# Two blocks of a transformer: half of the memory's values computed in another stage

## The reference, cut to what matters

```python
mx = split((silu_c @ w_mod[l] + b_mod[l]), 6)              # shifts, scales and gates of a layer
zx = modulate(rms_norm(x, norm1_g[l]), mx[0], mx[1]) @ w_in[l]
...                                                        # mixers, w_o
x  = x + mx[2] * mixer_rest(...)
hx = modulate(rms_norm(x, norm2_g[l]), mx[3], mx[4])       # the layer's second norm
x  = x + mx[5] * square(relu(hx @ w_mlp1[l])) @ w_mlp2[l]
...
# second block, much later
mem_n = rms_norm_2(mem, norm_mem)
kv = (mem_n @ xa_wkv).reshape(B, M, 2, 4, 256)             # keys: first 1024 columns, values: last 1024
```

## Time and profile before

| | us |
|---|---|
| median of 3 runs (lowest, highest) | 1874.79 (1873.02, 1876.01) |
| the profiled execution | 1872.94 |
| its span, from the first to the last instruction | 1871.1 |
| TensorE busy in the span | 1764.5 (94%) |
| VectorE, ScalarE, GpSimd busy | 925.8, 398.6, 298.0 |
| mean granted TensorE clock | 0.982 |

### The profile page before, as it was taken

How to read it: one execution, slowest core, us unless ns; L and a number is a source line. 1 busy time by engine, 2 the same in 40 slices (tenths; PEclk the granted TensorE clock), 3 DMA queues, 4 the chain that set the end, 5 groups by cost and what they waited for, 6 DMA issues and landing times.

```text
span 1871.1 us, 25901 instructions
## 1 busy us (share of the span) xinstructions
PE 1764.5 (94%) x10456; PEld 1391.1 (74%) x10456; DVE 925.8 (49%) x1738; ACT 398.6 (21%) x757; POOL 298.0 (16%) x305
## 2 busy tenths in 40 slices
PE   7999999899999999899899999977999899999997
PEld 5434444488888888656899987855798688888886
DVE  1247542464676434575687643299621432255511
ACT  1312444221112210346221002210421101200000
POOL 0100252122001211005243110166000000000000
PEclk9999999999999999999999999888999999999999
DMA  7774483122333222321354554222312344244443
GB/s 291 308 288 185 161 323 127 67 71 88 113 135 113 81 79 88 112 68 52 130 179 159 177 180 138 91 95 108 113 48 92 113 158 135 91 158 153 144 154 112
DMA packets 38704, 256.22 MB, mean 137 GB/s; under 512 B 4128, under 2 KB 7328, under 8 KB 9024
## 3 DMA queue, kind: packets, MB, share of 16 engines
q1 hardware_dynamic: 36240, 240.86, 36.9%
q0 software_dynamic: 1776, 9.57, 1.3%
q10 hardware_dynamic: 576, 4.19, 0.5%
HBM read 247.27 MB, written 7.34 MB: 136 GB/s over the span
## 4 chain that ended last, share of the span: by engine, by line
PE 78%; DVE 13%; ACT 2%; DMA 2%; issue 2%; POOL 2%; SPq 0%; ACTq 0%; DVEq 0%; POOLq 0%
PE ps L595 77%; DMA ring<-weights 1%; DVE arena L1869 1%; PE ps L790 1%; DVE arena L2027 1%; DMA xT<-x_t 1%; DVE arena L2067 1%; DVE spare L2140 1%; DVE arena L2066 1%; POOL aux L1672 0%; DVE aux L1899 0%; DVE arena L1900 0%; DVE arena L1901 0%; ACT hT L1322 0%; POOL aux L1655 0%
## 5 line engine op out<-in xcount | busy, mean ns | idle before, releaser
L595 PE MATMUL ps<-hT,ring 128*128 128x256 f32 (+3 forms) x3184 | 739.6, 390 | 22.7 <-issue 17.0
L595 PEld LDWEIGHTS ps<-hT,ring 128*128 128x128 f32 (+1 forms) x3184 | 571.3, 193 | 181.3 <-issue 111.2
L595 PE MATMUL ps<-arena,ring 128*128 128x256 f32 (+3 forms) x1884 | 380.2, 358 | 5.0 <-DVE arena L1901 3.2
L595 PEld LDWEIGHTS ps<-arena,ring 128*128 128x128 f32 (+1 forms) x1884 | 317.6, 190 | 58.7 <-issue 13.3
L1655 POOL TENSOR_TENSOR aux<-aux 128x256 f32<-128x256 f32 (+1 forms) x46 | 50.0, 1088 | 611.0 <-ACT aux L1257 543.0
L595 PE MATMUL ps<-arena,sums 128*128 128x256 f32 (+1 forms) x768 | 136.5, 327 | 1.3 <-DVE aux L1965 1.3
L595 PEld LDWEIGHTS ps<-arena,sums 128*128 128x128 f32 x768 | 118.2, 191 | 12.3 <-DVE aux L1965 2.5
L1257 ACT ACTIVATE aux<-xT 128x256 f32<-128x256 f32 (+1 forms) x64 | 31.0, 494 | 285.7 <-DVE xT L2057 93.3
L1672 POOL TENSOR_SCALAR aux<-aux,small 128x512 f32<-128x512 f32 (+1 forms) x48 | 70.8, 1483 | 117.8 <-DVE small L1917 117.7
L1691 POOL TENSOR_TENSOR arena<-arena 128x256 f32<-128x256 f32 (+1 forms) x32 | 27.0, 843 | 332.4 <-ACT arena L1442 332.4
L595 PE MATMUL ps<-hT,sums 128*128 128x128 f32 (+1 forms) x512 | 78.6, 301 | 0.7 <-DVE aux L1965 0.4
(11 more groups left out here) (334 smaller groups left out, 1831.8 us busy)
## 6 DMA issues: line engine op xcount, KB each, us to landing
ring<-weights SPq DMA_DIRECT2D x224, 1024.0 KB, 4.9
kept_turns<-aux ACTq DMA_DIRECT2D x4, 1024.0 KB, 5.7
arena<-kept_turns POOLq DMA_DIRECT2D x6, 512.0 KB, 4.6
kept_keys_values<-spare POOLq DMA_DIRECT2D x1, 2048.0 KB, 8.2
arena<-kept_keys_values POOLq DMA_DIRECT2D x1, 2048.0 KB, 8.1
tab<-tables SPq DMA_DIRECT2D x1, 1344.0 KB, 13.7
arena<-mem_t SPq DMA_DIRECT2D x2, 512.0 KB, 5.7
xT<-ctx_t SPq DMA_DIRECT2D x1, 1024.0 KB, 9.2
```

The costliest lines, as they stand in the source:

```text
L595: ins = nc.tensor.matmul(o_, lhsT, rhs, start=start, stop=stop, skip_group_check=True)
```

## The change

The last 512 columns of the values (`values(1)`) leave the opening stage. Their two chunks now stand between the last chunk of `w_o` and the first of layer 0's MLP. TensorE does them in three parts, behind tile 7 of `w_o` and in the two steps after it. In the opening stage `mod_block(0, 3)` now stands ahead of `values(0)`, and `mod_turn(0, 0)` and norm 0's statistic stand inside it. GpSimd adds four of the squares of norm 0 and TensorE takes the other four. ScalarE and VectorE take their steps in the order that this gives. The first half of the values and the keys are stored by two transfers (1 MB, and 0.5 MB in pieces of 2 KB). The late half is copied to free memory and stored by two transfers of ScalarE's queue. `ctmp` moves, so that the normalized memory stays whole until then.

```diff
-SUMMED = {0: 7, 1: 7, 2: 6, 3: 7, 4: 6, 6: 7, 7: 7, 8: 7}
+SUMMED = {0: 4, 1: 7, 2: 6, 3: 7, 4: 6, 6: 7, 7: 7, 8: 7}
...
     keys(6, 8)
+    mod(0, 3)
     values(0)
-    mod(0, 3)
-    values(1)
...
+        if l == 0:
+            whole()
+            values(1)
         whole()
         for what, hf, p, g, n in mlp_order(l):
...
-        ctmp = flat[:, o:o + 1024].rearrange("p (n t) -> p n t", n=2)
-        assert o + 1024 <= 16 * 1024
+        ctmp = flat[:, 4608:4608 + 1024].rearrange("p (n t) -> p n t", n=2)
+        assert o <= 56 * T
...
+        late_values = (rawf[:, 0:512], auxf[:, 6144:6656])
...
             mem_keys(6, 8)
-            mem_values(0, 0, KD)
+            mod_block(0, 3)
+            mem_values(0, 0, 2)
+            mod_turn(0, 0)
+            mem_values(0, 2, 4)
             for k in range(KD):
                 norm_stat_step(("st", 0), 0, k, slice(0, 2 * T))
-            mod_block(0, 3)
-            mem_values(1, 0, 2)
-            mod_turn(0, 0)
-            mem_values(1, 2, KD)
+            mem_values(0, 4, KD)
...
                     if n >= 2:
                         norm_stat_step(("st", 2 * l + 1), 2 * l + 1, n - 2, s)
+                    if l == 0 and n >= KD - 1:
+                        mem_values(1, *((0, 2), (2, 4), (4, KD))[n - KD + 1])
...
-                    did(f(first_v[:, tt * D + half * 512:tt * D + half * 512 + 512], bank(key), ACT.Copy), key=key, wait=False)
+                    if half == 0:
+                        did(f(first_v[:, tt * D:tt * D + 512], bank(key), ACT.Copy), key=key, wait=False)
+                    else:
+                        dst = late_values[tt]
+                        did(f(dst, bank(key), ACT.Copy), key=key)
+                        act.dma_start(kept[:, 2 + tt, 512:1024], dst).then_inc(S["values_kept"], 16)
...
-            mem_values_out(0)
-            root(("st", 0), rinv, slice(0, 2 * T), 1.0 / D)
...
             mod_rows_out(0, 0)
+            root(("st", 0), rinv, slice(0, 2 * T), 1.0 / D)
...
                     modulated(0, 0, 0, 0, (0, 1))
-                    mem_values_out(1)
+                    mem_values_out(0)
...
-                    act.wait_ge(S["mem_kept"], 16)
+                    act.wait_ge(S["mem_kept"], 32)
...
+                if l == 1:
+                    act.wait_ge(S["values_kept"], 32)
...
                 modulated_halves(l)
                 if l == 0:
+                    mem_values_out(1)
                     did(f(small2[:, 0, :], cols("s5_log_step_2", 0, S5T), ACT.Exp), "s5_act")
...
-            for half in range(2):
-                for tt_ in range(2):
-                    taken(pool, ("xv", half, tt_))
-            pool.dma_start(kept, spare[:, :, :]).then_inc(S["mem_kept"], 16)
-            pool.wait_ge(S["mem_kept"], 16)
+            for n in range(KD):
+                taken(pool, ("xk", n))
+            for tt_ in range(2):
+                taken(pool, ("xv", 0, tt_))
+            pool.dma_start(kept[:, 0:2, :], spare[:, 0:2, :]).then_inc(S["mem_kept"], 16)
+            pool.dma_start(kept[:, 2:4, 0:512], spare[:, 2:4, 0:512]).then_inc(S["mem_kept"], 16)
+            pool.wait_ge(S["mem_kept"], 32)
...
+            pool.wait_ge(S["values_kept"], 32)
             pool.dma_start(arena[:, 9:13, :], kept).then_inc(S["mem_back"], 16)
...
+            mods(0, 0, 0, 4 * MOD_FIRST)
             scaled(0, slice(0, 2 * T), ("st", 0))
-            mods(0, 0, 0, 4 * MOD_FIRST)
             for l in range(LAYERS):
                 s = side(l)
+                if l == 1:
+                    dve.wait_ge(S["values_kept"], 32)
```

More of the change, by code:

```diff
@@ L499, in two_blocks @@
                   "q_nope", "max_ready", "prob_ready", "sum_ready", "conv_scaled", "conv_done", "conv_centred", "conv_act", "hidden",
-                  "x1_square", "x1_root", "h2_ready", "s5_loaded", "mem_loaded0", "mem_loaded1", "mem_squares", "mem_ready", "mem_kept", "mem_back", "scaled",
+                  "x1_square", "x1_root", "h2_ready", "s5_loaded", "mem_loaded0", "mem_loaded1", "mem_squares", "mem_ready", "mem_kept", "values_kept", "mem_back", "scaled",
                   "gla_dve", "gla_act", "gla_done", "s5_act", "s5_dve", "s5_turn", "s5_tabs", "s5_scanned", "s5_states", "s5_spilled0", "s5_spilled1", "s5_back0", "s5_back1",
```

## The result

The changed kernel takes 1886.97 us (median of 4 runs, 1884.66 to 1889.3) against 1874.89 us (median of 4 runs as well, one more than were known before); the ratio is 1.0066, 95% interval 1.0054 to 1.0079. That is 12.1 us slower, where +9.8 was forecast with a range of 1879.8 to 1888.0. The profiled execution took 1888.15 us, 15.2 more than the one of before.

The account below looks back on a forecast made before the run. TensorE, busy 94% of the span, was taken as the bound, so its work and idle time count. Opening +0.6 and end of w_o +9.15 gave +9.8 us, 1884.6 as a median, range 1879.8 to 1888.0.

Parts of the forecast that it names:

- The opening's gap: Opening stage, behind the fourth w_mod block: TensorE idle 10.7 us from 50.9, until chunk 12 lands at 61.6.
- The clock's part: Opening, behind TensorE's long idle time: lower clock costs 2.0 us, between nothing and 2.7.
- The end of `w_o`: Layer 0, tile 7: VectorE's wait for chunk 68 and four additions delay the norm's chain and forms, +9.15 us.
- the third rival: End of w_o: VectorE not held by chunk 68, only TensorE's order counts; +6.2, in all +6.8, 1881.6; chance 0.07.
- some 5 us twice: Sign expected in the profile after: VectorE's L1941 waits some 5 us twice in `residual`.
- the start of the z tiles: Opening: first modulated tile at 79.8 doesn't bind; z tiles start at 83.0, 0.7 us earlier than before.
- The stores beside the chunk loads: z tiles: key and value stores compete with needed chunks, costing nothing to 2.5 us, taken as 1.3.
- +0.6: The opening's sum: -0.7 for the earlier z start, +1.3 for stores beside chunk loads.
- the second rival: Opening loses more: clock low for 5 us of full work, store takes its whole share; about +12, 1887; chance 0.10.

Follow-up runs that it names:

- tables_late: Changed kernel with SyncE's load of the tables (1.3 MB) behind chunk 13 instead of ahead of chunk 12; 1884.35 us, ratio 1.0053.
- fill_gap: Changed kernel with 20 extra matmuls in TensorE's gap behind the fourth w_mod block, into a bank later overwritten; one execution, 1888.16 us.
- hold_after_tile: Changed kernel with weight_sums of the MLP's second chunk behind the addition of w_o's tile 7 in layer 0; 1884.30 us, ratio 1.0051.
- gains_early: Changed kernel with VectorE forming the gain of layer 0's first norm ahead of the eight scaled tiles; 1882.52 us, ratio 1.0032.
- values_behind: Changed kernel with all late values behind the last statistic step and weight_sums of the second MLP chunk behind the scaled tiles; 1882.38 us, ratio 1.0033.
- both_repaired: Changed kernel with gain ahead of scaled tiles, all late values behind the last statistic step, second MLP chunk's weight_sums behind scaled tiles; 1874.46 us, ratio 0.9997.

## Why the prediction was right, point by point

**Which way, and why: right.** The opening's gap was forecast at 10.7 us from 50.9, and was 9.63 from 51.7. It is the queue ahead of chunk 12: tables_late moved it by the tables' share. The clock's part, taken as 2.0 us from a row of another stage, was 1.6 (5.32 against 3.68, and 3.70 in fill_gap).

**The end of `w_o`: right in place and nearly in size.** +9.15 was forecast and +8.45 came. The issue came 1.2 us behind the values' start, the landing took 4.7 us, and the four additions took 2.8, all a little under the rows used. The wait of VectorE's queue for chunk 68 was the mechanism. But it isn't alone: the order on TensorE by itself costs what the third rival said (+6.2; hold_after_tile came to +5.9). Two slips of the text change no sum: it announces a wait of VectorE of "some 5 us twice", where its own times give some 9 us for the second (4.98 and 9.90 came), and the MLP's first two chunks were one and two behind tiles 6 and 7, not both two.

**The step that failed: the start of the z tiles.** The forecast as a whole came true, but this step of it didn't. The text says that with one tile scaled and two modulations the first tile comes 5.8 us behind the statistic, at 79.8, and that this "doesn't bind". The modulations wait for `gain` as well, and VectorE forms that behind all eight tiles, 4.9 us of work. Before the change the same order stood there and cost nothing, because TensorE had values to do until 83.67; the earlier trace rows even name `gain` as what ended ScalarE's wait, and I read only the length of that row. The first modulated tile thus came at 85.6, not 79.8. That is 3.8 us of idle time and then a first z tile at the low clock, 10.10 us in place of 7.03. gains_early removes both.

**The term that was too large.** The stores beside the chunk loads were given 1.3 us. In the changed kernel TensorE waited for no chunk there, as z itself was late. With z at 81.2 the wait was 1.60 us, so there is such a wait and the term belongs to the kernel that I had in mind, not to this one. That kernel is gains_early: its place behind the z tiles (`mod_turn(0, 1)`) stands at 162.05 against 162.29, so -0.2 where +0.6 was forecast. In all the change's opening cost +5.2.

**Where the rest went.** By the trace the two places make +5.2 and +8.5, 13.7 together, and the median moved by 12.1. Between the z tiles and `w_o` this execution won back 3.0 us. That stretch (from `mod_turn(0, 1)` to the end of tile 7) took 188.3 to 194.7 us in the twelve profiled executions, with the same work in it, and was the second longest, 194.5, in the one of before. The rows account for 2.5 of the 3.0. At one place TensorE waits 1.05 us twice for VectorE in both kernels, and the eight records behind it took 5.23 us before and 3.70 after:

```profile
196.75 5.23 PE L595 MATMUL ps<-ring,arena 128*128 128x512 f32 x8 [1.05 <-DVE arena L1901]
...
270.66 1.06 PE L595 MATMUL ps<-ring,sums 128*32 128x512 f32 x6 [1.28 <-DMA ring<-weights]
```

```profile
201.89 3.70 PE L598 MATMUL ps<-ring,arena 128*128 128x512 f32 x8 [1.05 <-DVE arena L1918]
...
235.47 1.06 PE L598 MATMUL ps<-ring,sums 128*32 128x512 f32 x6 [0.32 <-DMA ring<-weights]
```

That is 1.5 us, at a granted clock of 0.83 from 190 to 200 us before and 1.00 in the changed kernel. Another 1.0 us is the wait for a chunk, 1.28 us before and 0.32 after. Nothing in the edit aims at either. Behind the first form product the trace adds 4.5 us (15.2 in all), and 3.1 us of the 15.2 come from which two executions were profiled. So 13.7 - 3.0 + 4.5 - 3.1 gives the 12.1 of the medians.

**How much of the hit is luck.** A good part. 1887 is the time of the second rival, but not by its mechanism: the clock was back at 1.00 from 65 on, and no store took its share. +9.8 came near 12.1 with a missing delay of 3.8 us and the slow tile behind it, against a term of 1.3 us too many, 0.7 us too many at `w_o`, and the 3 us that the stretch between gave back; what came behind `w_o` was in no term at all. The measured median lies 1 us inside the upper end of the range.

## What to carry to other kernels

Work that a norm's chain hides also hides the order in that chain: before taking it away, list every wait of the first instruction behind it, the small ones last in a queue included. Work moved into a stream with a ring of few slots pushes all later loads behind itself, so whoever waits for one of them on an in-order engine is held with all that is queued behind it. And a gap on TensorE is best filled behind the last matmul that somebody waits for, not ahead of it: the same 13.9 us of values cost 5.9 us with half of them in front of the statistic's last step (8.5 with VectorE's hold on top) and 3.8 us with all of them behind it.

## What the runs showed of the hardware

Short gaps of equal length cost a different amount each time. The gap before the form products was 2.52 us in the changed kernel and 2.54 us in hold_after_tile; the eight records behind it took 3.56 us in the one and 1.99 us in the other, and the granted clock from 386 to 388 and from 380 to 382, in that order, was:

```profile
386.00:388.00 2.00, 2.00 (x6) 1.58 (x5) 1.93 (x3) 1.34 (x2) 0.00 (x0) 0.50 0.36 135
```

```profile
380.00:382.00 2.00, 1.84 (x9) 1.64 (x10) 1.93 (x3) 1.61 (x2) 0.00 (x0) 1.00 0.69 262
```

The end of layer 1's mixer has a gap of 2.56 or 2.57 us in all twelve kernels, the one before included. The four records behind it took 1.98 us in four of them (before, gains_early, values_behind, both_repaired) and 3.15 to 3.45 us in the other eight. Even behind the two gaps of 1.05 us shown above the records were slow in three of twelve (5.22 to 5.40 us against 3.70). After 3.80 us of idle time before the z tiles the first tile was slow in all five kernels that had this gap (8.62 to 10.17 us, against 7.03). So a gap of some 2.5 us costs up to 1.7 us more in some executions (3.66 against 1.99, in fill_gap) and nothing in others, and one of 3.8 us cost something each time here. What decides between them isn't shown. It is enough to move the time of a whole kernel by more than 1 us where nothing was edited. In "TensorE: Matmul & The Clock Gate", Part 1, the Trainium skill has an idle array fall to half clock and come back after sustained work; the falls after 3.80 and 9.63 us agree.
